# State space layer: the turns of groups 1 to 6 written out on all five engines in place of loops with registers

## The reference, cut to what matters

```python
def ssd_mixer(u, conv_state, ssm_state, w_in, conv_w, conv_b, dt_bias, a_log, d_skip, norm_g, w_out):
    proj = u @ w_in                                   # z, xbc, dt
    ...
    xc = conv_b + sum(xpad[:, k:k + l] * conv_w[k] for k in range(CONV_W))
    xc = jax.nn.silu(xc)                              # x, B, C; 8 groups of 4 heads
    ...
    y, h_last = ssd_chunked(xs, dt, a, bm, cm, h0)    # scan over chunks of 128 tokens
    y = y + d_skip * xs
    gz = y * silu(z), normalised over each group
    return gz @ w_out, new_conv, new_ssm
```

## Time and profile before

| what | value |
|---|---|
| median of 3 runs | 2455.61 us (2452.45, 2455.61, 2458.88) |
| profiled execution | 2457.03 us, its span 2455.2 us |
| PE busy | 2413.4 us (98%) |
| DVE, ACT, POOL busy | 76%, 57%, 30% |
| turns 2, 3, 4 and 6 of the state space layer | 65.10 to 65.16 us each |
| turn 5 | 68.90 us |

### The profile page before, as it was taken

One profiled execution on the slowest core, in us unless ns is written; L12 is line 12 of the kernel. 1 busy time (PEld: TensorE's weight loads), 2 busy tenths in 40 slices (PEclk: granted clock), 3 DMA queues, 4 the chain that ended last, 5 costly groups with the idle time before them and its releaser, 6 DMA issues.

```text
span 2455.2 us, 50197 instructions
## 1 busy us (share of the span) xinstructions
PE 2413.4 (98%) x19713; PEld 2361.6 (96%) x19713; DVE 1854.5 (76%) x3054; ACT 1394.2 (57%) x2388; POOL 735.9 (30%) x675
## 2 busy tenths in 40 slices
PE   8999999999999999999999999999999999999998
PEld 8999999899999989999999999999999998999998
DVE  8979767978888888978876988875235438988875
ACT  7757553645555556757666767664223227767663
POOL 1222233444445532222223122224322321222222
PEclk9999999999999999999999999999999999999999
DMA  7777743123333325677765677763443334677762
GB/s 192 165 169 174 164 121 113 47 95 106 106 106 97 105 82 132 165 162 169 166 146 133 155 173 161 172 148 129 158 133 123 136 110 105 161 171 162 174 149 89
DMA packets 105686, 339.01 MB, mean 138 GB/s; under 512 B 13776, under 2 KB 17360, under 8 KB 87184
## 3 DMA queue, kind: packets, MB, share of 16 engines
q1 hardware_dynamic: 53936, 242.40, 29.9%
q0 software_dynamic: 51552, 93.87, 22.7%
HBM read 223.06 MB, written 19.32 MB: 99 GB/s over the span
## 4 chain that ended last, share of the span: by engine, by line
PE 90%; DVE 6%; issue 2%; ACT 1%; DMA 1%; DVEq 0%; SPq 0%; POOL 0%; POOLq 0%; ACTq 0%
PE ps L1641 17%; PE ps L1639 17%; PE ps L1649 17%; PE ps L1537 6%; PE ps L1545 6%; PE ps L1538 6%; PE ps L1658 2%; PE ps L1659 2%; PE ps L1666 2%; PE ps L1977 1%; PE ps L1979 1%; PE ps L1978 1%; PE ps L1588 1%; PE ps L1578 1%; PE ps L1579 1%
## 5 line engine op out<-in xcount | busy, mean ns | idle before, releaser
L1641 PE MATMUL ps<-sb_ual,sb_hw 128*128 128x288 f32 x2240 | 612.5, 295 | 0.0
L1639 PE MATMUL ps<-sb_uah,sb_hw 128*128 128x288 f32 x2240 | 609.1, 295 | 0.4 <-ACT sb_hr L1029 0.2
L810 POOL DMA_DIRECT2D sb_lw<-sb_rawf x328 | 283.0, 868 | 959.2 <-ACT sb_lw L984 942.5
L1639 PEld LDWEIGHTS ps<-sb_uah,sb_hw 128*128 128x128 f32 x2240 | 420.8, 188 | 1.0 <-issue 0.8
L1641 PEld LDWEIGHTS ps<-sb_ual,sb_hw 128*128 128x128 f32 x2240 | 421.1, 188 | 0.0
L793 POOL TENSOR_TENSOR sb_wl<-sb_raw,sb_wh 128x1024 fp32r<-128x1024 f32 (+1 forms) x106 | 262.3, 2475 | 410.6 <-ACT sb_wh L953 385.8
L1649 PE MATMUL ps<-sb_uah,sb_lw 128*128 128x288 f32 x2240 | 384.3, 293 | 0.6 <-DMA sb_lw<-sb_rawf 0.6
L1537 PE MATMUL ps<-sb_uh,sb_wh 128*128 128x288 f32 x1360 | 374.2, 302 | 0.7 <-DVE sb_zs L2719 0.6
L1538 PE MATMUL ps<-sb_ul,sb_wh 128*128 128x288 f32 x1360 | 367.3, 297 | 0.0
L1649 PEld LDWEIGHTS ps<-sb_uah,sb_lw 128*128 128x128 f32 x2240 | 327.9, 188 | 1.3 <-DMA sb_lw<-sb_rawf 0.8
L1537 PEld LDWEIGHTS ps<-sb_uh,sb_wh 128*128 128x128 f32 x1360 | 256.1, 188 | 8.3 <-issue 5.3
(11 more groups left out here) (366 smaller groups left out, 5115.1 us busy)
## 6 DMA issues: line engine op xcount, KB each, us to landing
sb_lw<-sb_rawf POOLq DMA_DIRECT2D x358, 256.0 KB, 3.6
sb_rawf<-w_ffn_in SPq DMA_DIRECT2D x87, 1024.0 KB, 5.1
sb_rawf<-w_ffn_so SPq DMA_DIRECT2D x32, 1024.0 KB, 5.1
sb_raw<-w_ssd SPq DMA_DIRECT2D x64, 512.0 KB, 3.6
sb_raw<-w_att SPq DMA_DIRECT2D x40, 512.0 KB, 3.9
sb_rawf<-w_ffn_out SPq DMA_DIRECT2D x32, 384.0 KB, 3.0
sb_h<-state SPq DMA_DIRECT2D x8, 1024.0 KB, 5.0
ssm_sample<-sb_h SPq DMA_DIRECT2D x8, 1024.0 KB, 4.8
```

Of the source, the lines that this page charges most:

```text
L810: pool.dma_start(slot(lw, p), rawf[:, s % 2, i * BL:(i + 1) * BL], accum_op=ALU.add).then_inc(ld_in[i], 16)
L1639: pe.matmul(out, w[:, k * P:(k + 1) * P], high[k], start=begins and k == 0, stop=False, skip_group_check=True)
L1641: pe.matmul(out, w[:, k * P:(k + 1) * P], low[k], start=False, stop=False, skip_group_check=True)
```

## The change

The loop over groups 1 to 6 becomes a Python loop on SP, POOL, ACT, PE and DVE. Every turn then has its own code with constant thresholds and addresses; the work instructions and their order stay. The register instructions and branches go. `Steps.loop` goes, and the choice of the unit in DVE's `back` is rewritten so that it gives the same numbers for integers.

```diff
     def wait(self):
-        self.eng.wait_ge(self.sem, self.base + self.n)
-
-    @contextmanager
-    def loop(self, first, last, per):
...
+        self.eng.wait_ge(self.sem, self.n)
...
                 store_conv(1)
-                with sp.Fori(1, GROUPS - 1) as g:
+                for g in range(1, GROUPS - 1):
...
                 group(0, True, False)
-                with pool.Fori(1, GROUPS - 1) as g:
+                for g in range(1, GROUPS - 1):
                     group(g, False, False)
...
-                with act.Fori(1, GROUPS - 1) as g:
+                for g in range(1, GROUPS - 1):
                     group(g, False, False)
...
-                with pe.Fori(1, GROUPS - 1) as g:
+                for g in range(1, GROUPS - 1):
                     group(g, False)
...
                 def back(g, m):
 
                     if m % 4 == 3:
-                        u = U_TAIL + 2 + m // 4 if isinstance(g, int) and g == GROUPS - 1 else None
-                        if u is None:
-                            u = U_TAIL + m // 4 if isinstance(g, int) else (g + 1) * 8 + (U_LOOP + 3 * (m // 4))
+                        u = (U_TAIL + 2 + m // 4 if g == GROUPS - 1 else U_TAIL + m // 4 if g == GROUPS - 2
+                             else (g + 1) * 8 + (U_LOOP + 3 * (m // 4)))
...
-                with self_.loop(1, GROUPS - 1, SSD_DVE_STEPS) as g:
+                for g in range(1, GROUPS - 1):
                     group(g, False, False)
```

More of the change, by code:

```diff
@@ L17 @@
-from contextlib import ExitStack, contextmanager
+from contextlib import ExitStack
 import numpy as np
@@ L124 @@
 NORM_OF_FFN = (0, 2, 3, 5)
-SSD_DVE_STEPS = 15
 QKV_ORDER = (2, 5, 8, 0, 1, 3, 4, 6, 7)
@@ L136, in __init__ @@
     def __init__(self, eng, sem):
-        self.eng, self.sem, self.base, self.n = eng, sem, 0, 0
+        self.eng, self.sem, self.n = eng, sem, 0
     def done(self, ins):
```

## The result

| | before | after |
|---|---|---|
| median of 12 runs each | 2460.44 us (2452.45 to 2464.76) | 2467.61 us (2461.97 to 2474.09) |
| span of the profiled execution | 2455.2 us | 2463.6 us |
| third taps that came second, turns 1 to 7 | 2 (turns 5, 7) | 5 (turns 2, 3, 4, 6, 7) |

The ratio is 1.0038, with an interval of 1.0027 to 1.0048: the written-out kernel is slower by 0.3 to 0.5%. The prediction had put at 0.3% the least difference that can be told from none, so the loss is of that size; its interval does not take in "no change". Two runs of the experiments lie far out (2909.54 us at a granted clock of 0.75 with the wait written out, 11455.84 us of the kernel before) and are in no ratio. The forecast was 2468.0 us.

The account below looks back on a forecast made before the run. PE's own work bounds the kernel, plus PE's stops when DVE's third tap loses to POOL. Base 2449.6 us + 12.6 us for six stops + 4 x 1.44 us of lower clock = 2468.0 us, range 2449 to 2473 us.

Parts of the forecast that it names:

- The mechanism: DVE's third tap and POOL's low part exclude each other; if DVE loses, PE loses 2.2 us at once.
- The cost of code and branches: Register work, branches and reading in code in turns 1 to 6: 0 for PE; return savings bounded at 0.8 us.
- The tap at 4.62: DVE's third tap begins 4.62 us into a written-out turn, as in turn 7 of before.
- The store at -2.74: SP's store of the sample states goes out 2.74 us before a written-out turn's start, against -2.65 in turn 7.
- POOL at 4.52: POOL's low part begins 4.52 us into a written-out turn, 1.13 us behind ACT's cast, first by 0.10 us.
- Six lost races: In each of turns 2 to 7 POOL begins before DVE's third tap; stops of 2.1 us each, 12.6 us.
- rival B: Race between tap and POOL goes both ways, three or four times lost: 2458 to 2464 us; chance 0.12.
- The clock in four of six: Behind four of the six stops PE's clock falls to its lower level, costing 1.44 us each.
- The base of 2449.6 us: The profiled execution of before, 2457.03 us, without its two lost races of 7.4 us.
- A: Rival: DVE wins the race everywhere, 2449.6 us, 6 us below the median of before; chance 0.14.
- C: Rival: nothing that matters moves, two lost races as now, 2454 to 2457 us; chance 0.06.
- D: Rival: reading code in stops engines at turn starts, 5 us on top, 2473 us or more; chance 0.06.

Follow-up runs that it names:

- the wait: POOL's first low part waits until DVE's third tap is done: 2453.92 us (0.9984) in the written-out kernel, 2451.98 us (0.9978) in the kernel before with loops.
- the late tap: Kernel before with its loops, plus one small DVE instruction ahead of the third tap: 2472.82 us, ratio 1.0051.
- two waits: POOL's wait for the third tap plus one in group 0 for DVE's scalings: 2452.73 us (0.9971) written out, 2449.69 us (0.9961) in loops.

## Why the prediction was right, point by point

**The mechanism**: right. The lead of POOL's low part, and not the work or the code, sets the time. Taking the race out of the written-out kernel gave 0.54% back; turning it against DVE in the kernel with loops cost 0.51%.

**The cost of code and branches**: right. Taken as 0; a turn of 2 to 6 without a lost race lasts 65.06 to 65.12 us written out and 65.06 to 65.21 us in loops. Here the Trainium skill, page "Runtime: NRT & Kernel Launch", section "Instruction fetch mechanics", would have unrolling save a fetch at each return of a loop. No run here shows that saving. The prediction says that the trace speaks against the rule; what the trace shows is that no fetch was seen at these returns, and not that their targets lay outside the window that the rule speaks of.

**The tap at 4.62**: right, 4.62 or 4.63 in all six turns. **The store at -2.74**: right, -2.72 to -2.78. **POOL at 4.52**: 4.54 to 4.58 in turns 2, 3, 4 and 6, 4.46 in turn 7, but 4.69 in turn 5. The step "the cast begins 6.13 us behind the store" failed. With SP alone written out the store moved by 0.14 us and the cast by nothing; in the kernel after the distance was 6.17 us in turn 2 and 6.33 in turn 5. Counting the two advances in full, 0.13 and 0.09 us, happened to land close to what all five engines together did. The decision was closer than the 0.10 us that I gave it: POOL led by 0.05 to 0.09 us in turns 2, 3, 4 and 6. And "whichever begins first runs" isn't exact by the records: a near tie goes to POOL, which the prediction had not counted.

**Six lost races**: five in the profiled execution. Turn 5 was won by 0.07 us, which is a piece of rival B. **The stop of 2.1 us**: right, 2.05 to 2.14.

**The clock in four of six**: two of five. Each fall made its turn some 1.5 us longer, as costed, but the share was too high. I had drawn it from two stops, of turns 5 and 7 of before, that both had a fall. Over all the profiled executions shown here the stops of this place were 2 in before, 5 in after, 4 with DVE alone, 1 with SP alone, 6 with the late tap and 5 with DVE and SP, 23 in all, and 11 had a fall right behind them.

**The base of 2449.6 us**: too low. It was the profiled execution less two races. The kernels without the race measured 2451.98 us in loops and 2453.92 us written out, 2.4 and 4.3 us more. The term above it was too high by as much: 18.4 us forecast, while the profile has 2.12 + 2.13 + 2.10 + 2.14 + 2.05 = 10.5 us of stops and two falls of 1.5 us, 13.5 us in all, and the ratios give 13.3 us. On the scale of the result, 2467.61 less those 13.3 is 2454.3 us without the race, 4.7 above the base. So 2468.0 came within 1 us of 2467.61 by two errors of 4 to 5 us that cancel. The forecast of the cause was good, that of the size was luckier than it looks.

**The distance to before**: forecast 12.4 us, measured 7.2 us by the medians and 9 us by the ratio. The 2455.61 us of three runs was a low draw: the kernel's twelve runs reach from 2452.45 to 2464.76 us, with a median of 2460.44. That three runs don't fix such a median could have been read from their spread of 6.4 us. The prediction read the distances between the three runs as races lost or won. The runs don't bear that out: with the wait, and so without the race, the kernel with loops still spreads over 7.1 us (2450.02 to 2457.08). How many races each run of before lost isn't known, since only one was profiled.

**The rivals.** A (DVE wins everywhere) would have had turns of 65.1 us throughout: only turn 5 was so. B (some races each way) had three or four lost and 2458 to 2464 us: five were lost, one was won. C would have left POOL at 4.76: it moved. D would have shown stops on PE that no engine released: there are none in the turns. In the kernel after PE also stops for 0.42 and 0.70 us in the feed-forward layers, for a load of sb_lw (at 1252.5 and 1629.8 us). Such stops don't go by the change: there are two of 0.80 and 0.83 us written out with two waits, but also one of 0.43 us in loops with one wait and one of 0.51 us with DVE alone written out, and none above 0.25 us in the written-out kernel with one wait.

## What to carry to other kernels

Where two engines exclude each other and the loser is the one on which PE waits, look at who comes first and by how much before touching either: an edit that saves 0.1 us off the critical path can lose 2 to 3.6 us on it. A lead of under 0.2 us should be made an order, with a wait that costs nothing, rather than left to the timing; here two lines took 0.2% off the kernel with loops, where writing the loops out cost 0.4%. They are no cure for the spread from run to run: 7.1 us in the 11 runs with one wait in loops, against 12.3 us in the 12 runs of before in the result; with both waits it was 5.0 us in loops and 7.7 us written out. In this kernel, where PE has its work queued, loops with registers cost nothing that shows, so writing them out bought nothing by itself.

## What the runs showed of the hardware

A near tie goes to POOL. The Trainium skill, page "SBUF — State Buffer", section "Who interferes with whom", says that the instruction that issues first holds the ports. By the start times in the records that holds from some 0.05 us on; below it the tap still lost and took 3.0 us, eight times in three kernels with a lead of 0.01 to 0.04 us for DVE, while all thirteen leads from 0.05 us on in turns 2 to 7 were won. If the rule holds, the starts in the records are not exactly the moments at which the ports are claimed; no run here shows that by itself.

Two of the stops in the kernel after are nearly equal in length, at the same place, and differ in the clock: of 2.13 us in turn 3 with 1.00 behind it, and of 2.14 us in turn 6 with 0.51 in the 3.5 us shown. What tells them apart isn't in the rows.
